# Expert stage of a hybrid encoder block: fixed weight order, one block per expert plus overflow, gate/up as split float32r

## The reference, cut to what matters

```python
x = x + jnp.matmul(merged, w_out[l])          # the output projection
h2 = rms_norm(x, g_ffn[l])
expert_id = g_idx[:, None] * EXPERTS_PER_GROUP + top_i        # 2 of 32 per token
weights = g_p * top_p
a = jnp.einsum('td,edf->tef', xb, w_eg)       # gate, w_eg (32, 1024, 256)
u = jnp.einsum('td,edf->tef', xb, w_eu)       # up
mid = jax.nn.silu(a) * u * cb[..., None]      # cb: 0 for experts not chosen
return jnp.einsum('tef,efd->td', mid, w_ed)   # down, w_ed (32, 256, 1024)
```

## Time and profile before

| | us |
|---|---|
| median of 3 runs | 1296.21 (1293.45 to 1296.26) |
| span of the profiled execution | 1294.0 |
| output projection ends | 821 |
| first `gate_up` matmul | 870.6 |
| last down matmul ends | 1284.2 |

### The profile page before, as it was taken

The page is one execution under the profiler, slowest core; times in us unless marked ns, Lnnn a source line. Parts: engine busy times, 40 slices in busy tenths (PEclk is TensorE's granted clock), DMA queues, the critical chain, the costliest instruction groups (busy, mean ns, idle before and its releaser), DMA issues.

```text
span 1294.0 us, 14232 instructions
## 1 busy us (share of the span) xinstructions
PE 1216.5 (94%) x5180; PEld 844.8 (65%) x5180; DVE 598.3 (46%) x922; ACT 302.9 (23%) x528; POOL 200.3 (15%) x246
## 2 busy tenths in 40 slices
PE   5999999999978999999999899759999999999996
PEld 5988888886645577776788788744444444444443
DVE  3338999993424454544466334551222222222222
ACT  3432111113433444444222111100101110110110
POOL 3010000000232332120000000021222222222222
PEclk8999999999969999999899999759999999999999
DMA  6011111110100000000420332179999999999991
GB/s 221 1 49 49 49 49 49 49 49 17 41 1 1 1 1 1 1 28 6 163 66 0 102 147 98 66 238 347 317 322 303 295 310 302 329 337 297 300 299 29
DMA packets 138979, 172.25 MB, mean 133 GB/s; under 512 B 12303, under 2 KB 119994, under 8 KB 138938
## 3 DMA queue, kind: packets, MB, share of 16 engines
q1 hardware_dynamic: 127866, 154.86, 36.2%
q0 software_dynamic: 11008, 16.82, 5.4%
q10 hardware_dynamic: 64, 0.02, 0.0%
HBM read 167.45 MB, written 27.26 MB: 150 GB/s over the span
## 4 chain that ended last, share of the span: by engine, by line
PE 87%; DVE 4%; ACT 3%; POOL 2%; issue 2%; DMA 1%; SPq 0%; DVEq 0%; POOLq 0%; ACTq 0%
PE pb L1431 19%; PE pb L1170 12%; PE pb L1171 12%; PE pb L1172 12%; PE pb L1448 10%; PE pb L1310 4%; PE pb L1287 4%; PE pb L1423 3%; PE pb L1299 2%; PE pb L1219 2%; PE pb L1229 1%; PE pb L1370 1%; PE pb L1181 1%; POOL ssh L479 1%; PE pb L1439 1%
## 5 line engine op out<-in xcount | busy, mean ns | idle before, releaser
L1431 PE MATMUL pb<-wgu,hgT 128*128 128x512 f32 x576 | 253.8, 594 | 0.0
L1431 PEld LDWEIGHTS pb<-wgu,hgT 128*128 128x128 f32 x576 | 109.8, 191 | 137.8 <-issue 137.8
L838 DVE SCALAR_TENSOR_TENSOR cv<-up,dwc,cv 128x1024 f32<-128x1024 f32 x120 | 154.1, 1284 | 3.7
L1170 PE MATMUL pb<-hT_hi,ws_hi 128*128 128x512 f32 x384 | 151.7, 395 | 0.0
L1172 PE MATMUL pb<-hT_hi,ws_lo 128*128 128x512 f32 x384 | 149.5, 389 | 0.0
L1171 PE MATMUL pb<-hT_lo,ws_hi 128*128 128x512 f32 x384 | 149.4, 389 | 0.0
L1448 PE MATMUL pb<-wed,midT 128*128 128x512 f32 x288 | 130.2, 595 | 0.0
L771 ACT ACTIVATE yb<-pb,wcol 128x512 f32<-128x512 f32 x36 | 24.7, 687 | 360.3 <-PE pb L1448 360.3
L1154 DVE COPY midT<-pb 128x256 f32<-128x256 f32 x36 | 15.3, 425 | 188.2 <-PE pb L1439 188.2
L1448 PEld LDWEIGHTS pb<-wed,midT 128*128 128x128 f32 x288 | 51.9, 190 | 52.0 <-issue 51.7
L531 POOL DMA_INDIRECT hg<-h_rows,icol x40 | 41.8, 1045 | 264.9 <-DVE icol L1144 244.4
(11 more groups left out here) (268 smaller groups left out, 1795.1 us busy)
## 6 DMA issues: line engine op xcount, KB each, us to landing
wgu<-in_w_e_gate SPq DMA_DIRECT2D x36, 1024.0 KB, 10.9
wgu<-in_w_e_up SPq DMA_DIRECT2D x36, 1024.0 KB, 17.1
wed<-in_w_e_down SPq DMA_DIRECT2D x36, 1024.0 KB, 14.5
ws_raw<-in_w_in SPq DMA_DIRECT2D x24, 512.0 KB, 3.7
xs<-in_x SPq DMA_DIRECT2D x8, 512.0 KB, 9.5
wout<-in_w_out SPq DMA_DIRECT2D x1, 4096.0 KB, 12.7
xb<-in_x SPq DMA_DIRECT2D x8, 512.0 KB, 5.0
h_rows<-h SPq DMA_DIRECT2D x8, 512.0 KB, 2.7
```

The costliest lines, as they stand in the source:

```text
L838: i = v.scalar_tensor_tensor(out=cv[:, c, :], in0=src, scalar=w, in1=cv[:, c, :], op0=ALU.mult, op1=ALU.add)
L1170: t_.matmul(out, w(0), m(0), start=start, stop=False)
L1431: m = t_.matmul(pb[:, GU_BANK[q % 2], :], hgT[q % 2][:, k, :], wgu[q][:, k, :], start=(k == 0), stop=(k == KD - 1))
```

## The change

- Blocks: block e is the first 128 rows of expert e, for all 32 experts, whether it has tokens or not. Rows past 128 go to overflow blocks 32 and up (`OVB = 16` at most, at least one trip of four is run). Only these read their expert's number from `bexp`.
- Loads: the weights of block 0 are issued once the last output projection matmul is done (`x1_ps`), ahead of the last store of `h2` and `x1`, those of blocks 1 to 3 right behind; nothing waits for the routing until block 32. Gate and up are read in row pairs, 2 KB contiguous instead of 1 KB.
- Gate/up: ScalarE rounds the landed weights to `wgu_hi` (two buffers, in two halves per block), VectorE writes `wgu_lo` over the raw weights; the gathered transpose is split in the same way out of PSUM. `gate_up` becomes 8 times `three`. It is cut in two halves around the `mid` transposes and `gather_T`.
- Because of the row pairs, `gather_T` reads columns of `hg` with a step of two.
- Gathers and the transposes past the last block are left out.

```diff
-    wgu = [place(f"wgu{i}", [P, KD, 2 * FF], F32, o) for i, o in enumerate(WO)]
+    wgu_raw = [place(f"wgu_raw{i}", [P, 2, KD, FF], F32, o) for i, o in enumerate(WO)]
+    wgu_lo = [place(f"wgu_lo{i}", [P, 2, KD, FF], F32R, o) for i, o in enumerate(WO)]
+    wgu_hi = [place(f"wgu_hi{i}", [P, 2, KD, FF], F32R, R1 + 16 * K * i) for i in range(2)]
...
+            def load_expert(b, e, used):
+                if used is not None:
+                    sp.wait_ge(gu_ps, used)
+                pair = "e (o p i) f -> p (e o) (i f)"
+                sp.dma_start(wgu_raw[b][:, 0, :, :].rearrange("p (o i) f -> p o (i f)", i=2), w_e_gate[0][bass.ds(e, 1), :, :].rearrange(pair, p=P, i=2)).then_inc(w_in0[b], 16)
...
             for j in range(NTILE + 1):
...
+                else:
+                    sp.wait_ge(x1_ps, NTILE)
+                    load_expert(0, 0, None)
...
+            for q in range(1, SLOTS):
+                load_expert(q, q, None)
+            with sp.Fori(0, NE // SLOTS - 1) as i:
+                for q in range(SLOTS):
+                    load_expert(q, i * SLOTS + (q + SLOTS), i * SLOTS + (q + 1))
+            sp.wait_ge(bexp_ok, 1)
...
+            def act_block(q, i, more):
+                nth = i * SLOTS + (q + 1)
+                act.wait_ge(gu_ps, nth)
+                a.activation(sil[:, :], pb[:, GU_BANK[q % 2], 0:FF], ACT.Silu).then_inc(sil_ok, 1)
+                if more:
+                    act.wait_ge(w_in0[(q + 2) % SLOTS], (i + (q + 2) // SLOTS) * 32 + 32)
+                    expert_hi(q + 2, 0)
+                    gathered_hi(q, i * SLOTS + (q + 3))
+                    expert_hi(q + 2, 1)
+                act.wait_ge(y_ps, nth)
+                act.wait_ge(wc_ok, nth)
+                a.activation(yb[q % 2][:, 0:512], pb[:, 4, :], ACT.Copy, scale=wcol[q % 2][:, :]).then_inc(y_a, 1)
...
+            def expert_lo(q, h, halves):
+                ks = slice(h * (KD // 2), (h + 1) * (KD // 2))
+                dve.wait_ge(gu_hi, halves)
+                v.tensor_tensor(wgu_lo[q % SLOTS][:, :, ks, :], wgu_raw[q % SLOTS][:, :, ks, :], wgu_hi[q % 2][:, :, ks, :].bitcast(F32), ALU.subtract).then_inc(gu_lo, 1)
...
+            def dve_block(q, i, more):
+                b, nth = q % 2, i * SLOTS + (q + 1)
+                dve.wait_ge(sil_ok, nth)
+                v.tensor_tensor(mid[:, :], sil[:, :], pb[:, GU_BANK[b], FF:2 * FF], ALU.mult).then_inc(mid_ok, 1)
+                if more:
+                    expert_lo(q + 2, 0, i * (2 * SLOTS) + (2 * q + 5))
+                dve.wait_ge(mt_ps, nth)
+                v.tensor_copy(midT[:, :, :], pb[:, 3, 0:FF].rearrange("p (f t) -> p f t", f=2)).then_inc(mt_ok, 1)
+                if more:
+                    gathered_lo(b, i * SLOTS + (q + 3), i * SLOTS + (q + SLOTS))
+                    expert_lo(q + 2, 1, i * (2 * SLOTS) + (2 * q + 6))
+                dve.wait_ge(y_out[b], i * (8 * SLOTS) + 16 * (q // 2 + 1))
...
-                    m = t_.matmul(pb[:, GU_BANK[q % 2], :], hgT[q % 2][:, k, :], wgu[q][:, k, :], start=(k == 0), stop=(k == KD - 1))
+                    m = three(pb[:, GU_BANK[q % 2], :], lambda s: hgT[q % 2][s][:, k, :], lambda s: (wgu_lo[q % SLOTS] if s else wgu_hi[q % 2])[:, :, k, :], k == 0, k == KD - 1)
...
+                    i = t_.transpose(banks(0, 2)[:, k * P:(k + 1) * P], cols[:, k // 2, k % 2, :], ident[:, :])
...
+            def pe_block(q, i, nxt, more):
+                if nxt:
+                    gate_up((q + 1) % SLOTS, i + (q + 1) // SLOTS, 0)
+                mid_T(q, i)
+                if more:
+                    gather_T(q % 2, i * (8 * SLOTS) + 16 * (q // 2 + 2), i * SLOTS + (q + 2))
+                if nxt:
+                    gate_up((q + 1) % SLOTS, i + (q + 1) // SLOTS, 1)
+                down(q, i)
```

More of the change, by code:

```diff
@@ L207, in build @@
     incl = small("incl", [P, NE])
[L208 to L210 removed]
+    shift = small("shift", [P, NE])
+    home = small("home", [P, NE])
+    rank = place("rank", [P, NTILE, NE], F32, ONO)
+    over = place("over", [P, NTILE, NE], F32, ONO + K)
+    cmp7 = place("cmp7", [P, NE, 7], F32, ONO + K)
     pos2 = small("pos2", [P, 2, NTILE])
@@ L410, in _ @@
                     sp.dma_start(out_v[j - 1], x1[:, j - 1, :]).then_inc(x1_out, 16)
[L412 to L432, removed]
+            for q in range(1, SLOTS):
[3 more added lines that the diff above has]
+                    load_expert(q, i * SLOTS + (q + SLOTS), i * SLOTS + (q + 1))
             sp.wait_ge(bexp_ok, 1)
-            with sp.Fori(0, ntrip - 1) as i:
+            ntrip = sp.value_load(ntrip_i[0:1, 0:1], min_val=1, max_val=OVB // SLOTS)
+            with sp.Fori(0, ntrip) as i:
                 for q in range(SLOTS):
-                    e = sp.value_load(bexp[0:1, bass.ds(i * SLOTS + (q + SLOTS), 1)], min_val=0, max_val=NE - 1)
-                    load_expert(q, e, i * SLOTS + (q + 1))
+                    e = sp.value_load(bexp[0:1, bass.ds(i * SLOTS + q, 1)], min_val=0, max_val=NE - 1)
+                    load_expert(q, e, i * SLOTS + (q + 1 + NE - SLOTS))
             sp.wait_ge(y_all, 2)
@@ L759, in _, with expert_hi @@
             a.activation(second[:, :], second[:, :], ACT.Exp).then_inc(r_exp, 1)
-            act.wait_ge(route_ok, 1)
-            ntrip = act.value_load(ntrip_i[0:1, 0:1], min_val=2, max_val=MAXB // SLOTS)
-            with act.Fori(0, ntrip) as i:
-                for q in range(SLOTS):
[L766 to L771, removed]
+            def expert_hi(q, h):
+                ks = slice(h * (KD // 2), (h + 1) * (KD // 2))
+                a.activation(wgu_hi[q % 2][:, :, ks, :], wgu_raw[q % SLOTS][:, :, ks, :], ACT.Copy).then_inc(gu_hi, 1)
@@ L774, in _ @@
+            with act.Fori(0, last) as i:
+                for q in range(SLOTS):
+                    act_block(q, i, True)
+            for q in range(SLOTS):
+                act_block(q, last, q < SLOTS - 2)
         @block.vector
@@ new lines, in _ @@
+            link(v.tensor_scalar(shift[:, :], shift[:, :], float(P), float((NE - 1) * P), ALU.mult, ALU.add))
+            link(v.tensor_tensor(shift[:, :], shift[:, :], home[:, :], ALU.subtract))
+            v.tensor_tensor(rank[:, :, :], ranks, row(home[:, :], NE), ALU.add)
+            link(v.scalar_tensor_tensor(out=over[:, :, :], in0=ranks, scalar=float(P), in1=row(shift[:, :], NE), op0=ALU.is_ge, op1=ALU.mult))
+            link(v.tensor_tensor(rank[:, :, :], rank[:, :, :], over[:, :, :], ALU.add))
@@ L1164, in _ @@
+            with dve.Fori(0, last) as i:
+                for q in range(SLOTS):
+                    dve_block(q, i, True)
+            for q in range(SLOTS):
+                dve_block(q, last, q < SLOTS - 2)
         @block.tensor
@@ L1440, in finish, with down @@
                 m.then_inc(mt_ps, 1)
-                gather_T(q % 2, i * (8 * SLOTS) + 16 * (q // 2 + 2))
+            def down(q, i):
+                nth = i * SLOTS + (q + 1)
                 pe.wait_ge(mt_ok, nth)
```

178 lines of the change are left out of this document (98 added, 80 removed).

## The result

The kernel after takes 1284.45 us (median of 4 runs, 1280.47 to 1286.77), before 1295.91 (1293.45 to 1296.26): ratio 0.991, 95% interval 0.9897 to 0.9924. That is 11.5 us faster, where 43 were forecast, and 6 us above the range. The profiled execution has a span of 1278.4 (its own time 1280.47, the fastest of the four).

What follows compares the result with a forecast made beforehand. TensorE was taken as the bound, with the DMA engines close behind. A gain of 51.1 us, less 1 (table), 1 (loads), 2 (start) and 4 (scatters), gave 43 us: a forecast of 1253 us, range 1242 to 1278.

Steps and rivals of the forecast that it cites:

- Part 1, gate/up: TensorE's gate/up as 24 float32r matmuls for 8 float32: 1.43 us less a block, pace 9.98, 51.1 us gained in all.
- Part 2, the splitting: Splitting on ScalarE and VectorE takes 9.4 us a block, hidden under 9.98; the Silu table load costs 1 us in all.
- Part 4, the start: First gate/up starts about 1 us later despite early loads, and the clock returns later for 1 more: 2 us lost.
- Part 5, the scatters: Chain of scatters, 10.3 us each against a pace of 9.98: lag left at the end costs 4 us, between 0 and 54.
- Part 3, the loads: Expert stage's DMA time, 9.9 us a block from packet prices or 10.4 scaled, against a pace of 9.98: 1 us lost.
- The estimated lead of 12 us: Weight loads in the expert loop run 12 us ahead of need; TensorE starves only after this is used up.
- DMA as the bound: Rival: DMA engines bound the expert stage at 10.4 to 11.1 us a block, costing up to 26 us, 1253 to 1278; chance 0.16.
- The prediction's own sign of being wrong: The prediction is wrong if one of two paces near 10 us, loads or scatters, lies above 11.
- The split chain: Rival: splitting on ScalarE and VectorE is 0.6 to 1.5 us a block longer than summed, up to 1284; chance 0.09.
- The slower rival: Rival: denser load lengthens scatter landings past 10.6 us, so the scatter chain sets the pace, up to 1303; chance 0.07.
- The strided `gather_T`: Rival: `gather_T` with a step of two costs up to 0.88 us more a block, 32 us, 1285; chance 0.04.
- Another trip: Rival: the expert loop needs another trip of four blocks beyond 36, costing 40 us, 1293; chance 0.02.

Runs made afterwards that it cites:

- the 8 KB kernel: Kernel after with gate/up of the next block issued before this block's down weights, and all expert weights in rows of 8 KB: 1276.83 us.
- the row runs: Kernel after with gate/up rows of 1 KB, of 4 KB, or of 4 KB with down rows of 8 KB: 1293.81, 1280.19 and 1276.14 us.

## Why the prediction was wrong

**What bounds before: right.** TensorE; shown by before with 2 KB rows.

The spans, in the sum's own terms (us gained, forecast and measured):

| | forecast | measured |
|---|---|---|
| start of the first gate/up product | -2 | 1.7 |
| gate/up products outside the 34 paces | 1.4 | 2.9 |
| the `gather_T` that fall away at the end | 1.1 | 1.0 |
| 34 paces (products, table, loads) | 48.6 - 2 | 8.2 |
| behind the last down projection | -4 | 1.8 |
| sum | 43 | 15.6 |

Half of block 1's gate/up moved from ahead of block 0's `mid` into the tail; its 2.8 us are left out of both rows that it touches. The paces fall 38.4 us short: 30 for the loads, the rest because TensorE's own pace is 10.26 and not 9.98. The other rows give 11 back, and 2.1 of these are a stage before that ended earlier in this execution.

**Part 1, gate/up: right, 0.13 us short.** An undisturbed block in the timeline of the kernel after, TensorE alone, from the `mid` transposes to the next first half:

```profile
949.25 0.38 PE L1495 MATMUL pb<-ident,mid 128*128 128x128 f32 x2
949.46 1.12 PE L1478 MATMUL pb<-ident,hg 128*128 128x128 f32 x8
950.34 0.47 PE L1224 MATMUL pb<-wgu_hi,hgT_hi 128*128 128x512 f32 x1
...
953.19 3.59 PE L1506 MATMUL pb<-wed,midT 128*128 128x512 f32 x8
956.22 0.79 PE L1224 MATMUL pb<-wgu_hi,hgT_hi 128*128 128x512 f32 x1
...
959.72 0.44 PE L1495 MATMUL pb<-ident,mid 128*128 128x128 f32 x2 [0.20 <-DVE mid L1196]
```

The second half takes 953.19 - 950.34 = 2.85, down 3.03, the first half, with the table's delay behind it, 3.50. Without that delay the pace is 10.11 against 9.98: the two cuts between kinds of matmul cost what a sum of equal matmuls doesn't have.

**Part 2, the splitting: right that it is hidden, wrong on the table.** The operations took 1.91 and 2.29 us as summed. The Silu table load (1.28 us) does not come back: it lengthens two paces in four from 10.11 to 10.48 and 10.29 (no down weights), since it stands between `yb` and `sil`, and TensorE then waits for `mid`. The mean is 10.22 to 10.26 where nothing else disturbs, so 4 to 5 us over 34 paces, where 1 was taken.

**Part 4, the start: 0.4 us later, where 2 was forecast.** The first gate/up product and the last down projection of the kernel after:

```profile
868.83 0.77 PE L1224 MATMUL pb<-wgu_hi,hgT_hi 128*128 128x512 f32 x1
...
1266.60 3.70 PE L1506 MATMUL pb<-wed,midT 128*128 128x512 f32 x8 [0.52 <-DVE midT L1200]
```

The first product starts 1.7 us earlier than before's (870.55), but the output projection had ended 2.1 us earlier in that execution (819.08 against 821.17), so from there it is 0.4 later, and 0 to 1.9 later in the other runs with the new start. `mid` of block 0 comes 7.4 us earlier for another reason. Before, the whole gate/up of blocks 0 and 1 stood ahead of it (885.19 - 870.55 = 14.64 us), now that of block 0 and the first half of block 1's (877.75 - 868.83 = 8.92). Of these 5.7 us some 2.8 are the half that moved behind `mid`, which the tail gives back, and 2.9 are the shorter products of two blocks. Part 1 counted 1.4 for block 0's and forgot block 1's, which lies outside the 34 paces too.

**Part 5, the scatters: no loss.** The 4 us did not come: from the end of the last down projection to the end of the span it is 8.1 us against 9.8 before. The last scatter lands after 4.5 us in place of 5.9; it now carries the few rows of an overflow block (0.06 MB against 0.27). The mechanism exists, as the 8 KB kernel shows, and begins to hold only when landings go to 10.3.

These errors cancel by luck. Without scatter rows the span is 1250.1, 43.9 less than before, where 43 were forecast. But its 34 paces give 34 x (11.41 - 10.26) = 39.1 where the sum had 46.6, since TensorE's own pace is 10.26 and not 9.98; 4.6 come from fewer and shorter products ahead of block 0's `mid`, and its last scatter has no rows to land.

**Part 3, the loads: the step that failed.** The sum had 9.9 us of DMA time a block against a pace of 9.98, and took 1 us. It measured 10.9 of busy time: weights 0.782 x 300/26.8 = 8.8 (summed at 8.1), rows 0.187 x 300/26.8 = 2.1 (summed at 1.8). The late blocks come every 11.54 us. The loss is 24 x (11.54 - 10.26) = 31 us.

Two packet prices were too low for this stage: 162 ns for 4 KB, and 86.5 for 2 KB, worked out from it and the 48.7 for 1 KB. They come from stretches of 8 and 2.5 us with loads alone. It is tempting to blame the scatters beside the loads, but the runs don't bear it out: without scatter rows the weights still take 0.856 x 300/29.3 = 8.8 us a block. In the expert stage the mean packet takes 92.9 ns at 2 KB and 189 at 4 KB (the figures in the expectations of the row runs); with these the weights come to 9.0. Why a 4 KB packet of weights takes 189 ns here and 162 there was not found out. The rows of before already held the warning: the same prices give before 6.2 + 2.6 + 1.8 = 10.6 us a block, and its whole stage showed 11.1, or 11.3 by the count of bytes above. The other end of the range, scaled from that stage to 10.4, was the better row. Its 0.7 for 2 KB rows holds: 11.3 becomes 10.6 in before with 2 KB rows, where TensorE does not wait. The kernel after, with its blocks closer together, has 10.9, and why a block then takes 11.54 from start to start was not taken apart.

The estimated lead of 12 us fits: at a deficit of 11.54 - 10.26 = 1.3 us a block it lasts 9 blocks, and the first long pace (13.0 us) is that from block 11 to 12. That lead hid the error only in part.

**The rivals.** What came is the first one, DMA as the bound, at 0.16 and 1253 to 1278; its upper end used 11.1 a block less the lead, and 11.5 was needed. The prediction's own sign of being wrong, a pace of the loads above 11, came with it. That a starved stage needs more than a covered one (11.54 against 11.41 with the same bytes) no row of before shows. The split chain, 9.21 us where products are few, was no bound. The slower rival, the chain of scatters, did not set the kernel after (see the run without gather rows), though it does so with 8 KB rows. The strided `gather_T` has a price, 0.07 to 0.09 a block and not 0.88. Another trip did not come: 36 blocks.

## What to carry to other kernels

When the DMA share beside a busy engine is 0.98, the DMA time of a block is already known: share times pace. A sum of packet prices has to give that time for the kernel before; where it does not (10.6 against 11.1 to 11.3 here), scale the measured time and do not trust the sum. Take from it only what the edit removes. What is left, 10.6 here, is a lower bound: the starved stage took 11.54 from block to block. A faster engine then gains the distance between the two paces (here nothing) plus the lead that the buffers hold (here ten blocks, 11.4 us). And once one of two close paces is relieved, look at the other: here loads, then the chain of adding scatters.

## What the runs showed of the hardware

- Adding on the way costs DMA time: 0.9 us a block for 0.23 MB, in a stage that then moves 322 instead of 353 GB/s.
- Larger rows are not free for others: from 4 to 8 KB in gate/up the weights stopped being late, but the scatters' landing went from 9.7 (4 KB rows, order of after) to 10.3 us and the kernel got 4 us slower.
- The eight transposes of `gather_T`, from their start to the next product in the kernel after and its variants, take 0.79 us without a step, 0.88 with a step of two or four, 0.81 with a step of eight. Why the price nearly goes away with the longer step was not explained.
- A stall of TensorE of 3.5 us was followed by a slower stretch: the down projection of 3.59 took 5.40 us, with a mean granted clock of 0.83 from 1030 to 1040 us, and 1.00 in the ten us behind.
- Mean time of a packet of weights in the expert stage: 50.0 ns at 1 KB (before), 92.9 at 2 KB and 189 at 4 KB (after), where short stretches with loads alone had 48.7 at 1 KB and 162 at 4 KB. Taking the scatters' rows out did not lower the weights' 8.8 us a block.
